# A conv's layer norm moved into its input run, modulation pieces spread anew, and four norms made by wide operations

## The reference, cut to what matters

```
shift, scale, gate = split(silu(c) @ ada_w[i] + ada_b[i], 3)
h  = rms_norm_2(x,   norm_g[i]) * (1 + scale) + shift
hc = rms_norm_2(ctx, norm_g[i]) * (1 + scale_c) + shift_c
```

```
a, a_gate, z = split(h @ w_in, 3)
g = a * sigmoid(a_gate)
y = depthwise_conv(g, 31 taps) + dw_b
y = silu(layer_norm(y, ln_g, ln_b))
out = (y * silu(z)) @ w_out
```

## Time and profile before

| | us |
|---|---|
| three runs | 3209.72, 3211.66, 3215.5 |
| median | 3211.66 |
| profiled execution, its own time | 3213.67 |
| its span | 3212.0 |
| TensorE busy in it | 3069.1 |

### The profile page before, as it was taken

The page is one execution under the profiler, slowest core; times in us unless marked ns, Lnnn a source line. Parts: engine busy times, 40 slices in busy tenths (PEclk is TensorE's granted clock), DMA queues, the critical chain, the costliest instruction groups (busy, mean ns, idle before and its releaser), DMA issues.

```text
span 3212.0 us, 58735 instructions
## 1 busy us (share of the span) xinstructions
PE 3069.1 (96%) x24402; PEld 2936.1 (91%) x24402; DVE 2399.6 (75%) x3318; ACT 1368.0 (43%) x1469; POOL 272.9 (8%) x530
## 2 busy tenths in 40 slices
PE   6999999999999899999999999999999999899998
PEld 6997889989978899999999998998798999799998
DVE  7877889978878888865675677677867976566464
ACT  4435453443345534433443335334734333434342
POOL 0000000000000000000000110100000422000000
PEclk9999999999999999999999999999999999899999
DMA  6874547768745577665767774865266765376563
GB/s 228 285 280 172 171 161 270 274 210 281 273 170 177 177 291 251 212 240 203 257 236 261 253 271 154 290 253 191 80 242 224 227 198 192 130 264 244 202 225 130
DMA packets 130953, 710.48 MB, mean 221 GB/s; under 512 B 16392, under 2 KB 16544, under 8 KB 71584
## 3 DMA queue, kind: packets, MB, share of 16 engines
q1 hardware_dynamic: 67392, 484.47, 43.1%
q0 software_dynamic: 61264, 214.93, 19.4%
q10 hardware_dynamic: 2064, 7.70, 0.7%
HBM read 700.26 MB, written 2.10 MB: 219 GB/s over the span
## 4 chain that ended last, share of the span: by engine, by line
PE 80%; DVE 11%; ACT 4%; issue 3%; DMA 2%; ACTq 0%; DVEq 0%; POOLq 0%
PE bank L526 24%; PE bank L522 21%; PE bank L523 21%; DVE wlo L1625 3%; PE bank L627 2%; DMA aslab<-w_ada_dram 2%; ACT whi L1062 2%; DVE aslab L1650 2%; PE bank L856 1%; DVE sc L1744 1%; PE bank L575 1%; PE bank L637 1%; PE bank L970 1%; PE bank L928 1%; PE bank L877 1%
## 5 line engine op out<-in xcount | busy, mean ns | idle before, releaser
L522 PE MATMUL bank<-uhi,whi 128*128 128x256 f32 x6720 | 1658.6, 287 | 54.7 <-issue 15.7
L523 PE MATMUL bank<-ulo,whi 128*128 128x256 f32 x6720 | 1643.1, 284 | 0.0
L1062 ACT CAST whi<-raw 128x2048 fp32r<-128x2048 f32 x456 | 867.6, 1905 | 1476.1 <-PE bank L526 1440.8
L1625 DVE TENSOR_TENSOR wlo<-raw,whi 128x2048 fp32r<-128x2048 f32 x456 | 1044.1, 2291 | 542.9 <-ACT whi L1062 542.0
L522 PEld LDWEIGHTS bank<-uhi,whi 128*128 128x128 f32 x6720 | 1298.5, 193 | 66.8 <-issue 50.6
L523 PEld LDWEIGHTS bank<-ulo,whi 128*128 128x128 f32 x6720 | 1298.8, 193 | 2.9 <-issue 2.4
L526 PE MATMUL bank<-uhi,wlo 128*128 128x256 f32 x6720 | 886.4, 284 | 11.0 <-DVE wlo L1625 11.0
L526 PEld LDWEIGHTS bank<-uhi,wlo 128*128 128x128 f32 x6720 | 841.7, 193 | 15.6 <-DVE wlo L1625 12.9
L466 POOL DMA_DIRECT2D aslab<-w_ada_dram x384 | 202.9, 528 | 2681.3 <-DVE mod L1650 1446.4
L1650 DVE CUSTOM_DVE_ANT_0 aslab<-aslab,sil,part 128x1024 f32<-128x1024 f32 x192 | 245.7, 1282 | 39.8 <-DMA aslab<-w_ada_dram 39.8
L1650 DVE CUSTOM_DVE_ANT_0 aslab<-aslab,sil,cols 128x1024 f32<-128x1024 f32 x192 | 245.5, 1281 | 39.0 <-DMA aslab<-w_ada_dram 39.0
(11 more groups left out here) (271 smaller groups left out, 2356.2 us busy)
## 6 DMA issues: line engine op xcount, KB each, us to landing
aslab<-w_ada_dram POOLq DMA_DIRECT2D x384, 512.0 KB, 5.2
raw<-w_win_dram SPq DMA_DIRECT2D x96, 1024.0 KB, 5.0
raw<-w_wfi_dram SPq DMA_DIRECT2D x96, 1024.0 KB, 5.0
raw<-w_wfo_dram SPq DMA_DIRECT2D x48, 1024.0 KB, 5.0
raw<-w_wci_dram SPq DMA_DIRECT2D x48, 1024.0 KB, 5.4
raw<-w_wo_dram SPq DMA_DIRECT2D x32, 1024.0 KB, 5.6
raw<-w_wpg_dram SPq DMA_DIRECT2D x32, 1024.0 KB, 5.1
raw<-w_wqz_dram SPq DMA_DIRECT2D x32, 1024.0 KB, 5.0
```

Source lines behind the costliest of these rows:

```text
L522: nc.tensor.matmul(o, w_, xhi_, start=start, stop=False, skip_group_check=True)
L523: nc.tensor.matmul(o, w_, xlo_, start=False, stop=False, skip_group_check=True)
L1062: nc.scalar.copy(whi[:, s % 2, 0:n], raw[:, s, 0:n]).then_inc(s_hi, 1)
L1625: v.tensor_tensor(wlo[:, s, 0:n], raw[:, s, 0:n], whi[:, s % 2, 0:n].bitcast(F32), ALU.subtract).then_inc(s_lo, 1)
```

## The change

- `ada_due` and the plan: `ga0` and `ga1` have 13 pieces in place of 16, one behind each of their first 13 slabs; `o0` 17 and `pg0` 18 in place of 16; `o1` 13 and `pg1` 14 in place of 12. In `o1` three pieces come first and ten from slab 7 on; `silu(3)`, which the pieces from 128 on need, moves from the end of `ple1` into group 1 of `o1`.
- The conv's layer norm: the mean is taken off right after its sum, under group 11; ScalarE squares after the roundings of slabs 2 and 3 of group 11; TensorE sums the squares behind slab 2 of that group; the silu, gate and split are made by chunks in turn, with slab 1 of `co` and the drain of group 11 behind the first two silu.
- The four norms: per chunk VectorE makes one product of 128 x 1024 with the reciprocal root, ScalarE four activations of 128 x 256 with scale and shift into `ulo_f` (a float32 view of `ulo`), waits for them, and rounds the chunk by one copy into `uhi`; VectorE makes the remainder of a chunk in one operation, behind the product of the next chunk.

```
-        run(f"ga{l}", "T", "win", 12 * l + 8, 4, ada=16)
+        run(f"ga{l}", "T", "win", 12 * l + 8, 4, ada=13)
         run(f"ple{l}", "E", "wple", l, 1, 4, 1024)
-        run(f"o{l}", "T", "wo", 4 * l, 4, ada=(16, 12)[l])
-        run(f"pg{l}", "T", "wpg", 4 * l, 4, ada=(16, 12)[l])
+        run(f"o{l}", "T", "wo", 4 * l, 4, ada=(17, 13)[l])
+        run(f"pg{l}", "T", "wpg", 4 * l, 4, ada=(18, 14)[l])
...
+        if r["name"] == "o1":
+            return min(p, 3) + 10 * max(0, p - 7) // 9
...
         def conv_squares(c):
-            return (sq[:, 0:1024], sq[:, 1024:2048], pt[:, :], sq[:, 0:1024])[c]
+            return (sq[:, 0:1024], sq[:, 1024:2048], pt[:, :], gp_t[:, 0:1024])[c]
...
-            group(r, 11, (r["e0"] + 11) % 2, slab_t)
+            def conv_square_sums(s):
+                if s != 2:
+                    return
+                for c in range(4):
+                    pe.wait_ge(s_lnq, c + 1)
...
+            group(r, 11, (r["e0"] + 11) % 2, slab_t, None, conv_square_sums)
```

ScalarE, in the norms' chunks and around the conv's layer norm:

```
                 def chunk(c):
                     act.wait_ge(s_slab, SLABS * RUN[next_run]["m0"] - (SLABS - 1) + c)
+                    act.wait_ge(s_nt, 16 * U_NORMS[name] + 4 * c + 4)
                     for kt in range(4 * c, 4 * c + 4):
-                        act.wait_ge(s_nt, 16 * U_NORMS[name] + kt + 1)
-                        nc.scalar.activation(uhi[:, kt, :], tt4[:, kt % 4, :], ACT.Identity,
-                                             bias=norm_shift(name, kt)).then_inc(s_nh, 1)
+                        nc.scalar.activation(ulo_f[:, kt, :], tt4[:, kt % 4, :], ACT.Identity,
+                                             bias=norm_shift(name, kt), scale=norm_scale(name, kt)).then_inc(s_ny, 1)
+                    act.wait_ge(s_ny, 16 * IN_RUN[name] + 4 * c + 4)
+                    nc.scalar.copy(uhi[:, 4 * c:4 * c + 4, :], ulo_f[:, 4 * c:4 * c + 4, :]).then_inc(s_nh, 4)
...
-                    silu(3)
...
-                    hooks=((1, second_block_inputs),) if l else ())
+                    hooks=((1, lambda: silu(3)), (1, second_block_inputs)) if l else ())
...
-                split(r, g, 2)
-                split(r, g, 3)
+                for s in (2, 3):
+                    split(r, g, s)
+                    if g == 11:
+                        for c in (2 * s - 4, 2 * s - 3):
+                            act.wait_ge(s_lnr, c + 1)
+                            nc.scalar.activation(conv_squares(c), yc_t[:, 1024 * c:1024 * c + 1024],
+                                                 ACT.Square).then_inc(s_lnq, 1)
...
+            split(RUN["co"], 0, 0)
+            act.wait_ge(s_lns, 2)
             nc.scalar.activation(sc[:, 0:T], bank[6][:, 0:T], ACT.Sqrt, bias=EPSB, scale=1.0 / D)\
                 .then_inc(s_cvr, 1)
...
+            conv_silu(0)
+            conv_silu(1)
+            split(RUN["co"], 0, 1)
+            drain_ci(r, 11, (r["e0"] + 11) % 2)
+            fill(0)
+            conv_silu(2)
+            fill(1)
+            conv_silu(3)
+            fill(2)
+            fill(3)
```

VectorE, in the norms' chunks and around the conv's layer norm:

```
+                def low(c):
+                    dve.wait_ge(s_nh, 16 * u + 4 * c + 4)
+                    t = slice(4 * c, 4 * c + 4)
+                    v.tensor_tensor(ulo[:, t, :], ulo_f[:, t, :], uhi[:, t, :].bitcast(F32), ALU.subtract)\
+                        .then_inc(s_nl, 4)
+
                 def chunk(c):
-                    for kt in range(4 * c, 4 * c + 4):
-                        normed(name, kt)
-                        if kt % 4 >= 2:
-                            normed_lo(name, kt - 2)
-                    normed_lo(name, 4 * c + 2)
-                    normed_lo(name, 4 * c + 3)
+                    if c:
+                        dve.wait_ge(s_ny, 16 * IN_RUN[name] + 4 * c)
+                    v.tensor_tensor(tt4, NORM_ARGS[name][0][:, 4 * c:4 * c + 4, :], r4, ALU.mult).then_inc(s_nt, 4)
+                    if c:
+                        low(c - 1)
+                    if c == 3:
+                        low(3)
...
+                if g == 11:
+                    dve.wait_ge(s_lns, 1)
+                    mu = sc[:, 512:768]
+                    link(v.tensor_scalar(mu, bank[5][:, 0:T], 1.0 / D, None, ALU.mult))
+                    mu4 = mu.unsqueeze(1).broadcast_to([P, 4, T])
+                    for c in range(4):
+                        y = yc[:, 4 * c:4 * c + 4, :]
+                        v.tensor_tensor(y, y, mu4, ALU.subtract).then_inc(s_lnr, 1)
...
+            conv_gate(0)
+            conv_gate(1)
+            split(RUN["co"], 0, 1)
+            fill(0)
+            conv_gate(2)
+            fill(1)
+            conv_gate(3)
+            fill(2)
+            fill(3)
```

More of the change, by code:

```diff
@@ L251, in build @@
         cql = tiles(sb("cql", 5 * T, F32R, at=place["sc"]))
+        ulo_f = tiles(sb("ulo_f", KT * T, at=place["ulo"]))
         XW = 516
@@ L329, in build @@
         s_nh = sem("normed_hi_ready")
+        s_ny = sem("shifted_tiles_ready")
         s_nl = sem("normed_lo_ready")
@@ L989, in _ @@
             last.then_inc(s_lns, 1)
-            group(r, 11, (r["e0"] + 11) % 2, slab_t)
[L992 to L997, removed]
+            def conv_square_sums(s):
[3 more added lines that the diff above has]
+                    pe.wait_ge(s_lnq, c + 1)
+                    for k in range(4):
+                        last = nc.tensor.matmul(bank[6][:, 0:T], ones[:, :],
+                                                conv_squares(c)[:, T * k:T * (k + 1)],
+                                                start=c == 0 and k == 0, stop=c == 3 and k == 3)
                 last.then_inc(s_lns, 1)
+            group(r, 11, (r["e0"] + 11) % 2, slab_t, None, conv_square_sums)
             project("co", "yco")
@@ L1032, in source_ready @@
                 eng.wait_ge(s_drain, 2 * (RUN[src]["e0"] + chunk + 1))
+        IN_RUN = {"nfc": 0, "nfx": 1, "nkc": 2, "nx1": 3}
         def norm_scale(name, kt):
@@ L1581, in _, with conv_silu @@
                 drain_ci(r, g - 1, (r["e0"] + g - 1) % 2)
-                split(r, g, 2)
-                split(r, g, 3)
+                for s in (2, 3):
[5 more added lines that the diff above has]
+                                                 ACT.Square).then_inc(s_lnq, 1)
                 if g in (3, 5, 7, 9):
                     conv_copy(g - 3)
[L1586 to L1595, removed]
+            split(RUN["co"], 0, 0)
+            act.wait_ge(s_lns, 2)
             nc.scalar.activation(sc[:, 0:T], bank[6][:, 0:T], ACT.Sqrt, bias=EPSB, scale=1.0 / D)\
                 .then_inc(s_cvr, 1)
[L1598 to L1603, removed]
+            def conv_silu(c):
+                act.wait_ge(s_lny, c + 1)
+                for kt in range(4 * c, 4 * c + 4):
+                    nc.scalar.activation(yc[:, kt, :], yc[:, kt, :], ACT.Silu, bias=col("conv_ln_b_2", kt),
+                                         scale=col("conv_ln_g_2", kt)).then_inc(s_lnz, 1)
+            fill = u_chunks("yco", yc_t, "co", lambda c: (s_yc, c + 1))
+            conv_silu(0)
[8 more added lines that the diff above has]
+            fill(3)
             run(RUN["co"], nothing, early="f3i")
@@ L1765, in norm_chunks @@
             def norm_chunks(name):
-                def chunk(c):
-                    for kt in range(4 * c, 4 * c + 4):
-                        normed(name, kt)
-                        if kt % 4 >= 2:
-                            normed_lo(name, kt - 2)
-                    normed_lo(name, 4 * c + 2)
-                    normed_lo(name, 4 * c + 3)
+                r4 = sc[:, 1024:1024 + T].unsqueeze(1).broadcast_to([P, 4, T])
+                u = U_NORMS[name]
+                def low(c):
[3 more added lines that the diff above has]
+                        .then_inc(s_nl, 4)
+                def chunk(c):
+                    if c:
[5 more added lines that the diff above has]
+                        low(3)
                 return chunk
@@ L2366, in _, with conv_gate @@
                 v.tensor_tensor(y, y, r4, ALU.mult).then_inc(s_lny, 1)
-            for c in range(4):
+            def conv_gate(c):
                 dve.wait_ge(s_lnz, 4 * c + 4)
-                if c == 0:
-                    dve.wait_ge(s_drain, 2 * (r["e0"] + 12))
+                dve.wait_ge(s_drain, 2 * (r["e0"] + 9 + c))
                 y = yc_t[:, 1024 * c:1024 * c + 1024]
                 v.tensor_tensor(y, y, zs_t[:, 1024 * c:1024 * c + 1024], ALU.mult).then_inc(s_yc, 1)
-            fill_u("yco", yc_t)
+            fill = u_chunks("yco", yc_t)
+            conv_gate(0)
[7 more added lines that the diff above has]
+            fill(3)
             run(RUN["co"], adder(h_t, lambda b: mods[:, 2, 0, 32 + b:33 + b]), early="f3i")
```

## The result

| | before | after |
|---|---|---|
| median of five runs, us | 3211.66 | 3226.29 |
| ratio, 95% interval | | 1.0050 (1.0037 to 1.0063) |
| profiled execution, span | 3212.0 | 3224.1 |
| TensorE busy in it | 3069.1 | 3077.6 |

The kernel is slower by 14.6 us in the medians and 12.1 in the spans; the prediction had +12.2 and 3224 (3210 to 3236).

A forecast was written before the change was run, and what follows sets the result against it. TensorE's work was 80% of the chain, so changes in its standstill count. Conv -8.3, gates -9, pieces +3, norms +22.4 and +4.1 sum to +12.2 us: 3225.9 on the profiled execution, forecast 3224 as median, range 3210 to 3236.

The forecast's parts named there:

- The ring: Norm fills: ScalarE and VectorE wait for each other in turns, 8.51 us against 6.64; +22.4 us over nfc, nfx, nkc.
- the lower end: Norm fills: if the activation stays at 504 ns, the three norms nfc, nfx and nkc cost 18.6 us, not 22.4.
- some 11 us a norm: Sign in the fills: TensorE stops for ScalarE three or four times per norm, some 11 us a norm.
- nkc with nx1: Norms in kvc: nkc +7.5 us by the ring; nx1, with two slabs less of lead, +4.1.
- The conv: Conv's layer norm: squares summed a slab earlier, so TensorE restarts before co sooner; -8.3 us, bounds -9.5 and -6.5.
- The gates' runs: `ga0` and `ga1`: one piece less in three slabs each shortens VectorE-bound stretches; -9 us, between -10.6 and 0.
- gates give nothing: Rival: gates' runs gain nothing and the moved pieces cost their upper bound; +23 us, 3235; chance 0.20.
- The six pieces: Pieces moved into pg0, o0, o1 and pg1: +3 us, between 0 and +6, with pg0's slab 7 the bad place.
- The stop near slab 8: In pg0, behind the double piece of slab 7: a late remainder stalls TensorE by 0.4 to 2.7 us.
- VectorE sets the pace: Rival: VectorE's own work paces the norm fills, so wide operations give -14.6 us, 3183; chance 0.14 with an unseen gain.

The follow-up runs named there:

- copy_twice: The kernel after with ScalarE's rounding copy of each norm chunk made twice; 3245.29 us, ratio 1.0101 to the kernel before.
- low_twice: The kernel after with VectorE's remainder of each norm chunk made twice, first into a scratch tile; 3229.77 us, ratio 1.0050 to the kernel before.
- product_ahead: The kernel after with VectorE's wide product of each chunk issued ahead of the slab's remainder; 3188.14 us, ratio 0.9924 to the kernel before.
- conv_alone: The kernel before with only the moved layer norm of the conv; 3204.21 us, ratio 0.9963.
- norms_alone: The kernel before with only the wide chunks of the four norms on both engines; 3241.0 us, ratio 1.0088.
- gates_ten: Narrow norms with next chunk's tiles ahead, moved conv norm, 19 pieces in `o0`, 16 in `pg0`, three more moved from `ga1` to `in1`; 3194.22 us, ratio 0.9937.
- pieces_alone: The kernel before with only the new counts of pieces and the new place of `silu(3)`; 3207.3 us, ratio 0.9981.
- all_but_norms: The kernel after with the narrow norm chunks of before on both engines; 3197.36 us, ratio 0.9954 to the kernel before.

## Why the prediction came out as it did, step by step

**The ring (+22.4).** The step held by its mechanism and by its size: a turn of 8.57 us against 8.51 worked out (its terms add up to 8.55), `nfc` and `nfx` +7.9 and +8.1 against 7.5. copy_twice and low_twice show that a step costs by its length if it stands in the ring, and nothing if it doesn't; product_ahead shows that with another order in VectorE's queue the same lengths cost nothing that can be told. The activation with scale and bias took 588 ns in the middle, so the lower end (504 ns, 18.6) is out. I gave "some 11 us a norm" for TensorE's stops; `nfx` has 8.7 and `nfc` 9.8.

**nkc with nx1 (+7.5 and +4.1).** Mis-sized: 14.2 measured. From the start of `fxo` to that of `qz` TensorE's stops grew from 7.9 to 17.6 us, by 9.8 and not by the 11.6 of the step, which had nothing for the clock. The other 4.4 us are matmuls that took longer. Busy times by stretch (us, then PE, PEld, DVE, ACT, POOL, granted clock, DMA share, GB/s) from the start of `kvc` to that of `qz`, in the kernel after and in the one before:

```profile
1965.40:2034.40 69.00, 54.26 (x370) 51.77 (x371) 38.26 (x30) 40.49 (x49) 1.05 (x2) 0.88 0.32 109
```

```profile
1948.80:2007.80 59.00, 52.14 (x389) 50.11 (x388) 42.96 (x67) 32.52 (x43) 1.05 (x2) 0.94 0.38 130
```

TensorE is busy longer for fewer matmuls. By the granted clock it was at its lower level (1.2 of 2.4 GHz) for some 17 us, and for 7 in the kernel before; without the parts that fell in a stop, 12 and 4. At half speed that is an estimated 4 of the 4.4 us. Not all of it need be the change's: conv_alone, which changes nothing there, is 3.6 us longer than before over the same runs.

**The conv (-8.3).** Right: -8.4 in the trace, -8.3 in that of conv_alone, -9 in its time. From the end of the squares' sums to the restart I had 13.2 us (13.0 if the last two figures, 2774.4 and 1.2, are added up rightly); the trace has 2797.99 - 2785.02 = 12.97.

**The gates' runs (-9).** Right in the place itself: -5.8 and -5.7, each a little over the bound of 5.3; with `ple1`, where the execution after lost 1.1 (norms_alone lost 1.4 there and conv_alone 1.1), -10.4. The stops for a maximum (2.27 us and one of 0.63) are gone from both runs. That is 2.9 of the 5.8; the clock, for which the step had nothing, can give up to 2 more (0.97 of 67 us before, 1.00 after). The same stretch as in the earlier trace rows, in the kernel after:

```profile
370.00:437.00 67.00, 65.01 (x492) 58.79 (x491) 63.68 (x174) 37.04 (x76) 3.69 (x7) 1.00 0.51 166
```

TensorE does 492 matmuls there and not 449, at a granted clock of 1.00 and not 0.97, and is now the busier of the two. The rival "gates give nothing" falls for the gates' runs themselves, and gates_ten shows that the bound has passed to TensorE, which that rival had feared one step too early. For layer 0 taken whole the rival was nearer: what `ga0` gains is lost again by `v1`. (That rival's sum takes 5 us for the moved pieces, where the step's own upper bound is 6.)

**The six pieces (+3).** In sum with the gates -6, and pieces_alone measured -6.0. But one sentence of the step was wrong: "after slab 15 of a run comes the next run's first remainder, which is made a slab ahead". In `pg0` it is followed by the drain of the last group, whose sum the next norm's squares wait for; it costs TensorE 1.89 us of the 3.3 in the table. The clock is 0.51 from 670 to 677 us:

```profile
670.00:677.00 7.00, 5.11 (x14) 3.62 (x13) 1.82 (x2) 5.09 (x5) 0.00 (x0) 0.51 0.81 305
```

But it fell there in the kernel before too: over the 27 us around the squares it is 0.79 (661 to 688) and was 0.81 (663 to 690), which is worth half a us. The rest of the 3.3 stays open. The stop near slab 8, foreseen as 0.4 to 2.7, was 1.65. That `silu(3)` costs nothing was not tried alone; layer 1, where it moved, gained.

**What was not in the sum.** The start and the spread of `qz` with the second attention. In all_but_norms, conv_alone and pieces_alone, none of which changes anything there, that stretch of `qz` differs from before by -3.5, -2.3 and -1.2 us, and all thirteen other traces are 1.2 to 6.0 us shorter there than the one of before. So the profiled execution of before was a long one there; why, stays open. The start is +1.2 and +1.0 us in conv_alone and norms_alone as well. In `f3i` the kernel before has stops of 1.11 and 2.14 us that the one after doesn't have; all thirteen other traces are shorter there, by 0.5 to 2.4, and nothing in the change touches it. So the close agreement of the total is in part luck: the norms came out at +30 in the trace and not +26.5, the first norm of `in1` lost 3.3 that I hadn't seen, and stretches without a term gave 5 back.

**VectorE sets the pace (-29)**, the rival on the other side: refuted by norms_alone, which was +28, and by low_twice. The Trainium skill, VectorE: DVE Perf Modes, The TRN2 errata, advises wide tiles because each instruction has a fixed cost. The trace agrees on the cost: four tiles 0.40 us apart became one operation with 1.13 us to the next. The time went the other way. Of the 1.9 us by which a turn grew, 0.7 are that ScalarE must wait for the whole product, where small tiles had flowed into it one by one; the other 1.2 are ScalarE's own, the rounding copy above all.

## What to carry to other kernels

When two in-order engines hand work to each other in turns, add up one whole turn of the ring and compare it with the time that the bound engine needs per step; neither engine's busy time tells it, and both may be idle for 4 us of 8.6. The cheapest cure is an order, not a shape: put the producer's next step in front of work that waits for the consumer (38 us here, with no operation changed). Before a piece of side work is moved, ask what stands behind it in its new queue, a drain included, and whether its loads can follow in that rhythm.

## What the hardware showed unasked

- The clock fell behind some stops of TensorE and not behind others of equal length. From the fills of `nfx` in the kernel after:

```profile
1647.80:1650.80 3.00, 2.96 (x25) 2.99 (x26) 3.00 (x2) 0.00 (x0) 0.00 (x0) 1.00 0.54 224
1656.30:1659.30 3.00, 2.94 (x14) 2.94 (x15) 2.96 (x3) 0.01 (x1) 0.00 (x0) 0.53 0.59 249
```

Behind a stop of 2.60 us it stayed at 1.00, behind the next, of 2.54 us, it was 0.53, and TensorE did 14 matmuls in 3 us and not 25.
- An activation of 128 x 256 with a scale and a bias per partition took 585 to 606 ns, 588 in the middle, in 64 cases; with the bias alone 504. Four in a row took 2.08 us, 0.50 apart.
